# A bidirectional mixing layer with a mixture of experts: the first adaLN vectors summed in four parts with three projection units accumulating behind them, and gate units with the activations stationary

## The chip, the cores and the metric

One core of a Trainium2 chip runs the whole layer. The metric is the device time of one execution in microseconds (us), the median of several runs. TensorE (PE) multiplies matrices, VectorE (DVE) and ScalarE (ACT) do elementwise work, GpSimd (POOL) helps in two places, and SyncE (SP) issues nearly all loads from HBM, in program order. TensorE's clock is granted at one of two levels, 1.2 or 2.4 GHz; the profile shows it as 0.50 or 1.00.

## The reference, cut to what matters

256 tokens, D = 2048, one layer, everything in float32.

```python
mod = c @ ada_w + ada_b                      # (1, 6*2048)
sh1, sc1, gt1, sh2, sc2, gt2 = split(mod, 6)
h = rmsnorm(x, norm1_g) * (1 + sc1) + sh1
u = h @ w_in                                 # columns: A 512, B 1024, C 1536, D 512, gates 4*2048
y_a = pool_mixer(u_A) * pool_scale; y_b = conformer(u_B); y_c = short_conv(u_C); y_d = fourier(u_D)
merged = sum_k sigmoid(gate_k) * y_k         # each y_k is 512 channels times a 512 x 2048 matrix
x = x + gt1 * (merged @ w_o)
h2 = rmsnorm(x, norm2_g) * (1 + sc2) + sh2
x = x + gt2 * moe(h2)     # 32 experts, top 2 of 8 in the best group of 4; w1, w3: 2048x512, w2: 512x2048
return rmsnorm(x, final_g)
```

## The kernel before

The order of the work on each engine is written out by hand, with a semaphore for each dependence; an engine's instructions and a queue's loads run strictly in the order in which they are written. `ring` is seven SBUF slots of 2 MB; loads of `w_in` and `ada_w` go through it.

**Head.** ACT issues sixteen small loads (`keep`, rows of norm and bias vectors, `c`), PE turns them into columns (L480 to L484), and SP's first `ada_w` load waits for the last of them. The vectors sh1 and sc1 are then made one after the other: SP loads `ada_w` in 16 tiles of 2 MB (two rows k of 2048 columns for each partition, runs of 8 KB), DVE multiplies each row by its element of `c` and adds it to `acc` (L1117, L1119: 16 instructions of 128x2048 for a vector), and PE sums `acc` over the partitions with 16 matmuls against ones (`sum_ada`, L503). Only when both vectors are there does ACT scale and shift `hT` (L913), 16 instructions, one for each 128 rows of the contraction.

**Projection units.** Seven units of 512 columns follow: five as `unit_T` (L523: the weights stationary, 256 tokens moving, output transposed), two as `unit_N` (L536: `hT` stationary, 512 columns of weights moving). A unit needs two tiles of `w_in` of 2 MB (eight rows of 512 columns for each partition, runs of 2 KB). A float32 matmul is recorded as two. DVE works behind them: more `ada_w` rows for gt1 and sh2, the 31-tap convolution (L1171, 120 instructions), the short convolution and a layer norm. Then come the DFT and the pooling on PE (L570 to L594).

**Gate units.** For each of four branches g, four units j of 512 gate columns in three fp32r products (high times high, high times low, low times high). `gate_unit` holds the weights stationary, `g_hi` for two of the three and `g_lo` for the third, and moves 256 tokens of `h_hi` or `h_lo` (L611, L613, L615): 192 matmuls a unit, in 8 pieces. For each piece ACT makes the high part of the weights (L975) and DVE the low part (L1242), three pieces ahead (`AHEAD`) and with four buffers for the high part. After a unit `gate_y` multiplies the branch's 512 channels with its output matrix (L587), DVE multiplies by the sigmoid and adds into `mergedT`. Meanwhile DVE sums further `ada_w` rows in tiles of 1 MB with two buffers (`ada_one`, L1234): sc2 during branch 0 (16 tiles over three units), gt2 during branches 1 and 2 (two tiles a unit). Branches 1 and 2 are one hardware loop (`Fori`) on every engine. SP's order is: a weight tile, two `ada_w` tiles, a weight tile, and so on.

**Output projection, router and experts.** `wo_products` (L686 to L688) multiplies `mergedT` with `w_o`, in 32 pieces, again three products; here the activations are stationary and 512 columns of weights move. The residual, the second norm and a router of many small steps on DVE follow. For the experts, the tokens are split into three bf16 parts (`xparts`, ACT L1020 and L1032, POOL L470) and gathered by matmul with 0/1 selection matrices (`gather`, L758: `xparts_k` stationary, read with a step of 16 elements). 32 passes, one for each expert; a pass loads 12 tiles of 1 MB (`in_exp_w`).

## Time and profile before

| | |
|---|---|
| median of 3 runs | 1986.92 us (1986.51 to 1989.77) |
| profiled execution | 1989.88 us; its span from first to last instruction 1988.1 us |
| busy | PE 1815.1 us (91%), DVE 729.1 us, ACT 424.3 us, POOL 16.8 us |
| DMA | 641.11 MB, mean 322 GB/s |
| mean granted clock of PE | 0.951 |

Read it by stages, since these have different limits: the head ends at 115.2 us, the third projection unit at 200.2, the seventh at 319.2, the first gate unit starts at 336.25, branch 0 ends at 459.2, branch 1 at 581.2, branch 2 at 710.6, branch 3 at 836.4, the output projection at 929.6, and the first pass of the experts starts at 994.0.

### The profile page before, as it was taken

The page shows a single profiled execution, that of the slowest core. Times are in us where ns is not written, and L with a number is a line of the kernel's source. Part 1 is how long each engine was busy: PE and PEld are TensorE (multiplying, and loading weights), DVE is VectorE, ACT ScalarE, POOL GpSimd, SP SyncE. Part 2 cuts the span into 40 slices and gives each one's busy share as a digit, 9 for nine tenths or more (in the row PEclk, how much of TensorE's full clock was granted, in tenths as well). Part 3 has the DMA queues.
Part 4 walks back from the last instruction along what each step waited for, and adds up shares of the span by engine and source line. Part 5 has one row for each costly group of instructions (what it writes and reads, how often), then busy time and mean ns, then how long its engine had stood idle before and what let it go on. Part 6 is the DMA issues. An engine that isn't in the chain of part 4 may idle for free.

```text
span 1988.1 us, 28852 instructions
## 1 busy us (share of the span) xinstructions
PE 1815.1 (91%) x11742; PEld 1233.8 (62%) x11742; DVE 729.1 (37%) x824; ACT 424.3 (21%) x506; POOL 16.8 (1%) x7
## 2 busy tenths in 40 slices
PE   1189999999999999997399999999999999999987
PEld 1178855998999999886245454544545445445444
DVE  5848855585545634444611111111111111111113
ACT  3020003332323323334111111111111111111112
POOL 0000000000000000000300000000000000000000
PEclk8589999998999999998699999999999999999999
DMA  8998676497565644455099999999999999999971
GB/s 364 419 367 329 239 294 250 156 399 292 218 249 206 259 170 170 160 194 208 5 380 422 422 422 422 422 422 422 422 422 422 422 422 422 422 422 422 422 333 64
DMA packets 128765, 641.11 MB, mean 322 GB/s; under 512 B 12944, under 2 KB 13380, under 8 KB 64196
## 3 DMA queue, kind: packets, MB, share of 16 engines
q1 hardware_dynamic: 127568, 638.12, 79.4%
q0 software_dynamic: 144, 1.70, 0.2%
q8 instruction: 46, 0.75, 0.1%
q10 hardware_dynamic: 996, 0.44, 0.1%
q14 instruction: 11, 0.09, 0.0%
HBM read 638.14 MB, written 2.10 MB: 322 GB/s over the span
## 4 chain that ended last, share of the span: by engine, by line
PE 70%; DMA 21%; DVE 6%; issue 1%; ACT 1%; ACTq 0%; SPq 0%; DVEq 0%
DMA ring<-in_exp_w 17%; PE ps L802 16%; PE ps L523 7%; PE ps L780 7%; PE ps L758 6%; PE ps L611 5%; PE ps L613 5%; PE ps L615 5%; PE ps L587 4%; DMA ring<-in_ada_w 4%; PE ps L536 3%; DVE r_m L1119 2%; PE ps L868 1%; PE ps L686 1%; PE ps L687 1%; PE ps L688 1%
## 5 line engine op out<-in xcount | busy, mean ns | idle before, releaser
L802 PE MATMUL ps<-ring 128*64 128x512 f32 x2048 | 468.1, 599 | 8.4 <-DMA ring<-in_exp_w 5.0
L802 PEld LDWEIGHTS ps<-ring 128*64 128x64 f32 x2048 | 151.1, 137 | 270.9 <-issue 265.7
L615 PE MATMUL ps<-h_hi,g_lo 128*128 128x256 f32 x1024 | 293.6, 287 | 0.0
L1481 DVE TENSOR_TENSOR r_c<-ps,scale 128x512 f32<-128x512 f32 x65 | 44.9, 691 | 535.4 <-PE ps L758 535.2
L758 PEld LDWEIGHTS ps<-r_c,xparts 128*128 128x128 bf16 x3120 | 199.6, 168 | 58.6 <-issue 51.1
L611 PE MATMUL ps<-h_hi,mix_hi 128*128 128x256 f32 x768 | 224.5, 292 | 6.8 <-DVE g_lo L1242 3.7
L613 PE MATMUL ps<-h_lo,mix_hi 128*128 128x256 f32 x768 | 221.3, 288 | 0.0
L758 PE MATMUL ps<-r_c,xparts 128*128 128x64 bf16 x3120 | 206.6, 228 | 7.3 <-ACT r_c L1034 5.2
L615 PEld LDWEIGHTS ps<-h_hi,g_lo 128*128 128x128 f32 x1024 | 200.6, 196 | 0.0
L975 ACT ACTIVATE mix_hi<-ring 128x1024 fp32r<-128x1024 f32 x96 | 101.3, 1059 | 276.1 <-PE ps L615 263.4
L611 PEld LDWEIGHTS ps<-h_hi,mix_hi 128*128 128x128 f32 x768 | 151.8, 198 | 8.2 <-DVE g_lo L1242 4.3
L1119 DVE SCALAR_TENSOR_TENSOR r_m<-ring,ccol,r_m 128x2048 f32<-128x2048 f32 x60 | 141.1, 2352 | 39.5 <-DMA ring<-in_ada_w 37.9
L1242 DVE TENSOR_TENSOR g_lo<-ring,mix_hi 128x1024 fp32r<-128x1024 f32 x96 | 117.2, 1225 | 98.8 <-ACT mix_hi L975 96.3
L613 PEld LDWEIGHTS ps<-h_lo,mix_hi 128*128 128x128 f32 x768 | 151.7, 198 | 0.4
L523 PE MATMUL ps<-r_h,ring 128*128 128x256 f32 x640 | 140.4, 383 | 1.4 <-ACT r_h L913 1.4
L1059 ACT ACTIVATE ring<-ps 128x512 f32<-128x512 f32 x64 | 34.7, 595 | 471.5 <-PE ps L780 471.5
L523 PEld LDWEIGHTS ps<-r_h,ring 128*128 128x128 f32 x640 | 122.9, 192 | 18.4 <-issue 1.4
L780 PE MATMUL ps<-ring,r_c 128*64 128x512 f32 x512 | 119.2, 607 | 3.1 <-DVE r_c L1498 3.1
L780 PE MATMUL ps<-r_b,r_c 128*64 128x512 f32 x512 | 116.9, 598 | 0.0
L1490 DVE TENSOR_TENSOR r_m<-ps,mod 128x512 f32 x64 | 41.2, 687 | 203.0 <-PE ps L790 203.0
L587 PE MATMUL ps<-r_b,ring 128*128 (+1 forms) x416 | 94.3, 384 | 0.3 <-DVE mod L1156 0.3
L780 PEld LDWEIGHTS ps<-ring,r_c 128*64 128x64 f32 x512 | 40.8, 139 | 79.9 <-issue 79.9
(247 smaller groups left out, 1675.4 us busy)
## 6 DMA issues: line engine op xcount, KB each, us to landing
ring<-in_exp_w SPq DMA_DIRECT2D x320, 1024.0 KB, 21.1
ring<-in_w_in SPq DMA_DIRECT2D x46, 2048.0 KB, 8.9
ring<-in_ada_w SPq DMA_DIRECT2D x32, 2048.0 KB, 11.8
r_b<-in_exp_w SPq DMA_DIRECT2D x64, 1024.0 KB, 21.2
ring<-in_ada_w SPq DMA_DIRECT2D x32, 1024.0 KB, 9.0
ring<-in_w_o SPq DMA_DIRECT2D x8, 2048.0 KB, 7.6
ring<-in_branch_w SPq DMA_DIRECT2D x6, 2048.0 KB, 10.7
r_m<-in_x SPq DMA_DIRECT2D x1, 2048.0 KB, 12.9
```

The costliest lines, as they stand in the source:

```text
L523: last = mm(u[:, f, :], w[:, kk, f * P:(f + 1) * P], hT[:, k, :], start=(k == 0 and f % 2 == 0), stop=(k == KT - 1), skip_group_check=True)
L536: last = mm(ps[:, u_bank(n) + t, :], hT[:, k, t * P:(t + 1) * P], w[:, kk, :], start=(k == 0), stop=(k == KT - 1))
L587: last = mm(y[:, f, :], lhs(k, f), rhs(k), start=(k == 0), stop=(k == kts - 1))
L611: mm(u[:, f, :], hi[:, o:o + P], h_hi[:, k, :], start=(k == 0 and f % 2 == 0), stop=False, skip_group_check=True)
L613: mm(u[:, f, :], hi[:, o:o + P], h_lo[:, k, :], start=False, stop=False, skip_group_check=True)
L615: last = mm(u[:, f, :], lo[:, o:o + P], h_hi[:, k, :], start=False, stop=(k == KT - 1), skip_group_check=True)
L758: last = mm(gat[:, kk, :], xparts_k[:, i, t, k, :], sel_e[:, t, :], start=(t == 0 and i == 0), stop=(t == TT - 1 and i == 2))
L780: last = mm(ps[side * NWIN:(side + 1) * NWIN, 4 + b, :], hid[:, f, :], chunk(CHUNKS + f)[:, q * MIX:(q + 1) * MIX], start=(f == 0), stop=( ...
L802: last = mm(ps[m * NWIN:(m + 1) * NWIN, 2, :], xe[:, k, :], chunk(2 * c + m)[:, kk * F:(kk + 1) * F], start=(k == 0), stop=(k == KT - 1))
L975: A(g_hi[x % 4], slot(q % W_SLOTS)[:, (x % 4) * 1024:(x % 4 + 1) * 1024], ACT.Copy).then_inc(g_hi_done, 1)
L1119: ins = V.scalar_tensor_tensor(out=acc, in0=w[:, i, :], scalar=ccol[:, kk:kk + 1], in1=acc, op0=ALU.mult, op1=ALU.add)
L1242: V.tensor_tensor(g_lo[:, q, (x % 4) * 1024:(x % 4 + 1) * 1024], slot(q)[:, (x % 4) * 1024:(x % 4 + 1) * 1024], g_hi[x % 4].bitcast(F32), ...
```

## The change

1. **Small loads.** The host lays out all small vectors as columns; ACT issues three small loads and the load of x. SP's first instruction is an `ada_w` load, with no wait. The transposes of the small vectors go.
2. **The first shift and scale in four parts.** sh1 and sc1 are made for 512 columns at a time: for each part, SP loads four `ada_w` tiles of 2 MB (eight rows of 512 columns, runs of 2 KB) and then three `w_in` tiles of 1 MB (four rows of 512 columns). DVE runs 32 instructions of 128x512 for a part, PE sums, DVE adds the bias, ACT modulates four k, and PE adds these four k to three projection units, held in PSUM at once.
3. **What follows in the projection.** Four units are left. gt1 is made there (8 tiles of 2 MB), sh2, sc2 and gt2 are made one in each of branches 0, 1 and 2, 16 tiles of 1 MB each, four in a unit.
4. **Gate units.** `h_hi` and `h_lo` are stationary and 512 columns of weights move: 96 matmuls a unit. `gate_y` likewise moves 512 columns. The merged result therefore stands with the tokens on the partitions, and is turned on PE (`turn_merged`, 8 transposes for each j) before the output projection. `pool_scale` is multiplied into `pool_w` on DVE (128x2048), which the first `gate_y` waits for. The row of gt1 is made in two halves.
5. **Loops.** PE, DVE and SP write branches 1 and 2 out; ACT keeps its loop.
6. **Gather.** `xparts` is written with a step, so that `gather` reads 128 neighbouring elements.

```diff
-            sp.dma_start(x_in, x_v).then_inc(x_loaded, 16)
-            sp.wait_ge(const_in, 16 * 16)
-            for n in range(ADA0):
-                if n >= ADA_FIRST:
-                    sp.wait_ge(acc_step, 2 * (n - ADA_FIRST + 1))
-                load_ada(n // 8, n % 8, 3 + n % ADA_FIRST, ada_in[n % ADA_FIRST])
+            def load_head(part, v, half):
+                i = 4 * part + 2 * v + half
+                if i >= ADA_FIRST:
+                    sp.wait_ge(acc_step, 8 * (i - ADA_FIRST + 1))
+                sp.dma_start(slot(3 + i % ADA_FIRST).rearrange("p (k n) -> p k n", k=8),
+                             ada_v[:, 8 * half:8 * half + 8, v * D + part * PART:v * D + (part + 1) * PART]
+                             ).then_inc(ada_in[i % ADA_FIRST], 16)
+            for part in range(4):
+                for v in range(2):
+                    for half in range(2):
+                        load_head(part, v, half)
+                for n in range(HEAD):
+                    load_head_w(part, n)
+            load_unit(3, 0)
...
+            load_gt1(2)
+            load_gt1(3)
+            load_gt1(4)
             gate_w(0, 0)
...
+            for part in range(4):                       # PE
+                head_sums(part)
+                for n in range(HEAD):
+                    u = tiles((0, 4, 2)[n])
+                    for kk in range(4):
+                        k = 4 * part + kk
+                        if n == 0:
+                            pe.wait_ge(h_ready, k + 1)
+                        for f in range(4):
+                            last = mm(u[:, f, :], head_w(i)[:, kk, f * P:(f + 1) * P], hT[:, k, :], ...)
+                    last.then_inc(head_used, 1)
...
-                        for f in range(4):
-                            o = kk * MIX + f * P
-                            mm(u[:, f, :], hi[:, o:o + P], h_hi[:, k, :], ...)
-                            mm(u[:, f, :], hi[:, o:o + P], h_lo[:, k, :], ...)
-                            last = mm(u[:, f, :], lo[:, o:o + P], h_hi[:, k, :], ...)
+                        cols = slice(kk * MIX, (kk + 1) * MIX)
+                        for t in range(TT):
+                            h = h_hi[:, k, t * P:(t + 1) * P]
+                            mm(ps[:, b + t, :], h, hi[:, cols], start=(k == 0), stop=False)
+                            mm(ps[:, b + t, :], h, lo[:, cols], start=False, stop=False)
+                            last = mm(ps[:, b + t, :], h_lo[:, k, t * P:(t + 1) * P], hi[:, cols], ...)
...
-                            last = mm(gat[:, kk, :], xparts_k[:, i, t, k, :], sel_e[:, t, :],
+                            last = mm(gat[:, kk, :], xparts[:, i, t, k * P:(k + 1) * P], sel_e[:, t, :],
...
-            A(xparts[:, 0, :, :], xn2, ACT.Copy).then_inc(parts_act, 1)
+            A(xparts_q[:, 0, :, :, :], xn2_q, ACT.Copy).then_inc(parts_act, 1)
...
+                for vec in range(2):                    # DVE, for each part
+                    total = head_acc(part, vec)
+                    for k in range(KT):
...
+                            ins = V.scalar_tensor_tensor(out=total, in0=w, scalar=ccol[:, k:k + 1], in1=total, ...)
+                        ins.then_inc(acc_step, 1)
+                        v.wait_ge(acc_step, 32 * part + 16 * vec + k + 1)
...
-            ADA_AT = {8 + 3 * k // 2: (k,) for k in range(16)}
...
+                    if i % 2 == 1:
+                        ada_one(0, 4 * j + i // 2)
                 if j == 0:
-                    save_mod(SH2, y_bank(n))
+                    v.wait_ge(bw_in, 16)
+                    v.wait_ge(ps_in, 16)
+                    V.tensor_tensor(slot(BW)[:, 0:2048], slot(BW)[:, 0:2048], slot(BW)[:, 2048:4096], ALU.mult
+                                    ).then_inc(pw_ready, 1)
...
-            with v.Fori(1, N_BRANCH - 1) as g:
+            for g in range(1, N_BRANCH - 1):
                 branch_gate(g, False)
...
+                    if g == N_BRANCH - 1 and j > 0:     # PE
+                        turn_merged(j - 1)
+            pe.wait_ge(row_saved, 1)
+            gate_row(1)
+            pe.wait_ge(row_saved, 2)
```

## Rows read from the trace of the kernel before

**Rows 1.** Busy time by stage: length, PE, PEld, DVE, ACT, POOL, clock, DMA share, GB/s.
```profile
40.00:85.00 45.00, 6.96 (x32) 6.90 (x32) 36.47 (x18) 0.00 (x0) 0.00 (x0) 0.50 1.01 422
95.00:116.00 21.00, 7.74 (x34) 7.62 (x35) 13.21 (x8) 1.53 (x4) 0.00 (x0) 0.50 1.04 388
115.20:200.20 85.00, 84.98 (x385) 74.55 (x386) 55.92 (x81) 9.55 (x17) 0.00 (x0) 0.98 0.85 335
200.20:319.20 119.00, 119.00 (x434) 80.25 (x433) 80.54 (x98) 8.16 (x11) 0.00 (x0) 0.99 0.76 291
319.20:336.25 17.05, 13.73 (x48) 8.74 (x46) 5.91 (x6) 10.89 (x11) 0.00 (x0) 1.00 0.66 248
336.25:459.20 122.95, 117.33 (x865) 115.10 (x865) 82.89 (x67) 40.16 (x39) 0.00 (x0) 0.92 0.68 262
459.20:581.20 122.00, 121.97 (x897) 118.29 (x896) 66.33 (x48) 37.54 (x36) 0.00 (x0) 0.98 0.62 236
581.20:710.60 129.40, 126.60 (x928) 123.19 (x928) 69.20 (x50) 37.54 (x36) 0.00 (x0) 0.97 0.62 234
710.60:836.40 125.80, 125.55 (x905) 120.33 (x905) 49.71 (x41) 42.25 (x40) 0.00 (x0) 0.98 0.42 155
836.40:929.60 93.20, 89.60 (x386) 73.02 (x384) 50.53 (x49) 32.77 (x31) 0.00 (x0) 0.98 0.53 194
1520.00:1920.00 400.00, 393.76 (x2745) 195.22 (x2741) 59.62 (x93) 65.35 (x93) 0.00 (x0) 1.00 1.01 422
```

**Rows 2.** Timeline of the head: start, length, engine, line, operation [idle before it].
```profile
13.64 1.91 ACT L898 ACTIVATE r_b<-r_m 128x2048 f32<-128x2048 f32 x1 [2.35 <-DMA r_m<-in_x]
...
70.98 35.78 DVE L1119 SCALAR_TENSOR_TENSOR r_m<-ring,ccol,r_m 128x2048 f32<-128x2048 f32 x15
```

**Rows 3.** Groups of DVE and ACT by form: count, busy us, mean ns, idle before.
```profile
L1119 DVE SCALAR_TENSOR_TENSOR r_m<-ring,ccol,r_m 128x2048 f32<-128x2048 f32 x60 | 141.1, 2352 | 39.5 <-DMA ring<-in_ada_w 37.9 <-DVE r_b L1171 0.2
L1457 DVE SCALAR_TENSOR_TENSOR r_c<-r_m,rs,r_c 128x512 bf16<-128x512 f32 x2 | 1.5, 751 | 0.1
L1242 DVE TENSOR_TENSOR g_lo<-ring,mix_hi 128x1024 fp32r<-128x1024 f32 x96 | 117.2, 1225 | 98.8 <-ACT mix_hi L975 96.3
L975 ACT ACTIVATE mix_hi<-ring 128x1024 fp32r<-128x1024 f32 x96 | 101.3, 1059 | 276.1 <-PE ps L615 263.4
```

**Rows 4.** Timeline: neighbouring matmuls of a gate unit (256 columns), then of the output projection (512).
```profile
342.05 0.28 PE L615 MATMUL ps<-h_hi,g_lo 128*128 128x256 f32 x1
342.17 0.28 PE L611 MATMUL ps<-h_hi,mix_hi 128*128 128x256 f32 x1
...
884.33 0.39 PE L686 MATMUL ps<-mix_hi,m_hi 128*128 128x512 f32 x1
884.56 0.39 PE L687 MATMUL ps<-g_lo,m_hi 128*128 128x512 f32 x1
```

**Rows 5.** Chain of waits within branch 0: start, length, what.
```profile
404.06 2.36 DVE r_m L1234
406.44 7.94 DMA ring<-in_ada_w
```

**Rows 6.** Chain of waits where the loop goes from branch 1 to branch 2.
```profile
574.26 6.91 PE ps L587 x32
581.17 2.82 issue
...
585.00 0.21 PE ps L611
```

**Rows 7.** Timeline from the second norm to the first gather.
```profile
938.83 3.62 ACT L1020 ACTIVATE xparts<-r_b 128x4096 bf16<-128x4096 f32 x1
...
938.94 5.10 PE L715 MATMUL ps<-keep,r_b 128*128 128x128 f32 x32 [9.31 <-ACT r_b L1016]
...
960.63 7.93 POOL L470 TENSOR_TENSOR xparts<-r_b,xparts 128x4096 bf16<-128x4096 f32 x1 [8.49 <-ACT xparts L1032]
...
981.65 3.23 PE L758 MATMUL ps<-r_c,xparts 128*128 128x64 bf16 x48 [5.25 <-ACT r_c L1034]
```

More of the change, by code:

```diff
@@ L65, with build @@
 N_MIXC = 1024 * 3 + 256
-def build(nc, x, c, ada_w, ada_b, norm1_g, w_in, pool_w, pool_scale, conf_dw_w, conf_dw_b, conf_ln_g,
-          conf_ln_b, branch_w, sc_conv_w, w_o, norm2_g, rg_w, rg_b, re_w, re_b, exp_w1, exp_w3,
-          exp_w2, final_g, keep_consts, mix_consts, iota_const, out):
+def build(nc, x, ada_w, w_in, pool_w, pool_scale, branch_w, w_o, rg_w, re_w, exp_w1, exp_w3, exp_w2, final_g,
+          columns, router_b, keep_consts, mix_consts, iota_const, out):
     with ExitStack() as ctx:
@@ L342, in gate_w @@
+            load_unit(3, 0)
+            load_unit(3, 1)
+            load_unit(4, 0)
+            load_gt1(0)
+            load_unit(4, 1)
+            load_gt1(1)
+            for n in (5, 6):
+                for half in range(2):
+                    load_unit(n, half)
             def gate_w(g, x):
                 q = G0 + x
-                if isinstance(g, int) and x < W_SLOTS and g == 0:
-                    sp.wait_ge(w_used, q - W_SLOTS + 1)
+                if x < W_SLOTS and g == 0:
+                    sp.wait_ge(w_used, q - 6)
@@ L496, in _ @@
             acc_k = acc.rearrange("p (q k) -> p k q", k=KT)
-            def sum_ada(n, bank):
-                pe.wait_ge(acc_step, 16 * (n + 1))
-                for k in range(KT):
-                    part = acc_k[:, k, :] if n == SH2 else acc[:, k * P:(k + 1) * P]
-                    last = mm(ps[:, bank, k:k + 1], part, ones[:, 0:1], start=True, stop=True)
-                last.then_inc(summed, 1)
-            pe.wait_ge(xT_saved, 8)
-            sum_ada(SH1, 2)
-            pe.wait_ge(mod_ready, 1)
@@ L509, in _, with head_sums @@
-            sum_ada(SC1, 2)
-            def unit_T(n, loaded):
+            def head_sums(part):
+                for v in range(2):
+                    pe.wait_ge(acc_step, 16 * (2 * part + v + 1))
+                    for kk in range(4):
+                        o = 16 * v + 4 * part + kk
+                        last = mm(ps[:, 6 + v, o:o + 1], head_acc(part, v)[:, kk * P:(kk + 1) * P], ones[:, 0:1],
+                                  start=True, stop=True)
+                    last.then_inc(summed, 1)
@@ L595, in _ @@
             last.then_inc(dft_done, 1)
+            pe.wait_ge(acc_step, ADA1)
+            for k in range(KT):
+                last = mm(ps[:, 6, k:k + 1], acc[:, k * P:(k + 1) * P], ones[:, 0:1], start=True, stop=True)
+            last.then_inc(summed, 1)
             def gate_unit(g, j):
-                u = tiles(u_bank(N_UNIT + j))
+                b = u_bank(N_UNIT + j)
                 for i in range(GATE_PIECES):
@@ L1601 @@
         a = _np.asarray(given[name])
-        if name not in ("final_g", "branch_w"):
+        if name not in ("final_g", "branch_w", "columns", "router_b"):
             a = a[0]
```

524 lines of the change are left out of this document (261 added, 263 removed).

## The prediction

> **What bounds the kernel now.** I read the stages first, then the timeline of the head, then the chain of waits inside the gate units, and last the experts.
>
> The stages [rows 1] show four different limits. In the head the core loads at full rate (DMA share 1.01) while PE has 6.96 us of work in 45: nothing multiplies until both vectors exist. From 115.2 to 319.2 us PE is busy without a gap, so there the number and length of its matmuls is the limit, and DVE and DMA have room. In branch 0 the DMA share and DVE's load are high and the clock is 0.92; the chain alternates between an `ada_w` tile that takes 7.94 us to land and the 2.36 us that DVE spends on it, 10.3 us for two tiles [rows 5]. In branches 1 to 3 PE is busy all the time again, except where the loop turns: 2.82 us of issue, and then matmuls of 0.21 us where a full clock gives 0.12 [rows 6, 4]. In the experts DMA stands at share 1.01 and 422 GB/s with PE at 393.76 of 400 us [rows 1]: a pass loads 12 tiles of 1 MB, 12.58 MB, and at 422 GB/s that is 29.8 us. So the expert stage ends a fixed time after its first loads can start; a faster PE there gives nothing, and whatever is won must be won before it.
>
> **Head and projection: 46 us.** *Loads.* Up to the last `ada_w` tile of part four there are 16 tiles of 2.097 MB and nine `w_in` tiles of 1.049 MB, 43.0 MB, all in runs of 2 KB. Runs of 2 KB went at 388 GB/s where they were alone at a full queue (95 to 116 us), runs of 8 KB at 422 [rows 1]. I take 388: 110.8 us. Ahead of or between them come x and the constants, 4.2 MB, 10 us, and a start at 1 us: the last tile lands at 122, the first of part four at 106. *DVE.* An instruction of 128x2048 takes 2.352 us, 15 of them 35.78, a gap of 0.03 [rows 2, 3]; one of 128x512 took 0.751 [rows 3]. 32 a part at 0.78 are 25.1 us, 100 in all, against 74 before: more DVE work, because each instruction is a quarter as long but carries the same fixed part. x landed at 13.6 us beside one other load [rows 2]; now three queues share, so I put it at 15.5 and the first sum at 20, after ACT's two squares (1.91 each) and two small steps. Parts one to three then wait for tiles (a part's 11.5 MB take 29.7 us, DVE 25 and 2 for the exchange with PE), so part four starts when its tile lands, 106, and ends at 131. *Hand-over.* Four sums at half clock 1.7 (6.96 for 32 records [rows 1]), three small DVE steps 0.7, one ACT instruction 0.6: PE starts at 134. *PE.* 48 matmuls, 96 records, at 85.0/385 = 0.221 us [rows 1]: 21.2 us. After the idle time some of it will run at half clock; the loop's turn cost 5.8 us of which 2.8 were idle, so about 3 [rows 6]; I take 2.5. Three units are done at 157.5. Before it was 200.2, so 42.7 us. Parts one to three are hidden: PE's 24 us fit into 29.7. The `w_in` tiles of a part reuse slots that PE freed two parts, some 50 us, earlier (`head_used`), so SP is not held up there, and the tiles of the fourth unit land by 150.
>
> By the Trainium skill ("DMA: Bandwidth & Descriptors", Specifications) transfers of 512 B and more run at line rate, so runs of 2 KB should cost nothing. The rows at 388 and 422 speak against it, and I keep the measured rate; what the rule would make of the time stands among the rivals.
>
> *Rest of the projection.* 119.0 us before, of which 3.5 (half of 6.96, at the full clock) were the sum for gt1, which moves behind the DFT: 115.5. Then 17 us of DFT and pooling as before, in whose last 3.3 us PE waited for the first pieces, and the moved sum fits there. The first gate unit starts at 157.5 + 115.5 + 17 = 290 instead of 336.25: 46 us. DVE's work here: convolution from 6 us before the third unit's end, 49 us, done before PE asks at 55; then five and three gt1 tiles of 4.8 us with two buffers, each refilled in about 7.6 us, done 111 us after the third unit, 5 before PE's last unit ends. Those 5 us are the cover; SP's `gate_w(0, 0)` and `gate_w(0, 1)` stand behind `load_gt1(4)` and `load_gt1(6)` and come with 15 us to spare. If the chain is late, the split of h waits (`acc_step`, ADA1) and the first gate unit with it, one for one.
>
> **Gate units.** The spacing of matmuls is 0.12 us for 256 columns and 0.23 (0.227 over longer stretches, 87 us for the 384 of the output projection) for 512 [rows 4]. A unit goes from 192 x 0.12 = 23.0 to 96 x 0.227 = 21.8. The form with 512 columns and stationary activations is the one that the output projection already runs, so both prices are of the same products. `gate_y` stays at 6.9 us [rows 6] (16 matmuls of 256 or 8 of 512), 1.7 in branch 0.
> *Branch 0:* 4 x (21.8 + 1.7) = 94. The scaling of `pool_w` is new: DVE comes to it after piece 7 of the first unit, ACT's 1.06 and DVE's 1.23 for one piece more [rows 3], an `ada_w` row 2.35 and the scaling itself, twice 1.225: 7.2 us, of which PE's last piece covers 2.7. PE waits 4.5, and after it and at the start about 2.3 each at half clock; behind it stand `gate_y` and the next unit. The final sum 3.5: 107 in all. Could the tiles hold it up as before? Two tiles now fall on four pieces and half a `gate_y`, 11.7 us, where the chain needs 10.3 [rows 5]; before they fell on three pieces. So PE sets the pace by 1.4 us per pair. 123.0 to 107: 16 us.
> *Branches 1 and 2:* 4 x (21.8 + 6.9) + 3.5 = 118.3 each, against 122.0 and 129.4 [rows 1]: the second loses the loop's turn as well (5.8). 14.8 us. DVE has eight pieces, four rows and 2.4 of merging, 21.8 us, in 28.7; the loads 9.4 MB, 24 us at 388.
> *Branch 3:* 114.8, three times eight transposes at 5.10/32 [rows 7], 1.3 each, half the row of gt1 1.7: 120.4 against 125.8, 5.4 us.
> *Output projection:* 93.2, less 1.2 of waiting for the merged result, plus the second half of the row 1.7, its copy 1.3 before PE may go on, a turn 1.3: 96.3, a loss of 3. SP's loads of router weights now wait for this row, and the fourth `w_o` tile stands behind them; it comes some 8 us later and was some 16 early, so nothing.
>
> **Gather, router, experts: nothing.** The two gathers ahead of the first pass take about 3.2 us each [rows 7], where 48 x 64 columns at the lower clock of 1.2 GHz alone are 2.6: at most 1.2 us to win. The copies into `xparts` now write with a step: ACT's 3.62 us, POOL's 7.93 twice [rows 7]. POOL's second subtraction ends at 968.6 and the first gather starts at 981.65, since it also waits for the selection: 13 us of cover. Below: minus 1.2. Above: ACT twice as long, 3.6 on the path to the router, and POOL half as long again, 4 us twice, which its cover holds. I take nothing. In the Trainium skill the page "SBUF — State Buffer" (Door 1: The DMA port swizzle, the note on 16-byte lines) says that an access which goes to a new line each time pays. That speaks for the gather and against the copies, and no row here shows an ACT or POOL write with a step; by it the sum would be 4 us worse.
>
> **Sum.** 46 + 16 + 14.8 + 5.4 - 3 = 79.2. The profiled execution, 1989.9 (span 1988.1), would be 1910.7; it lay 3 us above the median of the runs, so the median goes from 1986.9 to **1908**.
>
> **The rivals.**
> 1. *The loads of the head run at 422* (the rule above, as a mechanism of this kernel: 43.0 MB in 102 us). Then DVE binds: 20 + 4 x 25.1 + 3 x 2 = 126 instead of 131, and the result is 1903. For it: other stretches reach 422; against it: the 21 us at 388. 12%.
> 2. *Branch 0 keeps the pace of its loads.* The 1.4 us of room per pair go when the `w_in` tile ahead of each pair is slower or DVE comes late; PE then waits and falls to half clock, as in [rows 1], 0.92. Its 16 us are not won: 1924. For it: the chain before is just this, and 16 rows must now be done in a branch that has 17 us less. 14%.
> 3. *The copies with a step cost.* 4 to 8 us, 1914. 10%.
> 4. *gt1 comes late* at the end of the projection, by 5 to 10 us beyond its cover: 1915. 6%.
> 5. *PE stays at half clock in the head*, because it works in bursts: 96 x 0.427 = 41 us a part and 3 of exchange, more than the loads' 29.7, so the three units end at 47 + 4 x 44 = 223 instead of 157.5, and the result is 1974. Against it: the units began at full clock at once after 7 us of small sums, and the bursts are 70% of the time. 3%.
> 6. *Slower than before: the gather's new weight reads cost more, not less.* It is in every pass, 96 matmuls of 0.067 us at the first one [rows 7]. The loads cover up to 0.5 us a pass [rows 1]; to lose 79 us over 31 passes takes 2.5 more, so the point is 0.10 us a matmul. At 0.13 a pass is 35.5 us, 5.7 over the loads, and the result 2085. No row speaks for it but that the form is not in the trace. 3%.
> That the change does not do what it says would be head matmuls waiting for all four parts; the waits on `h_ready` and `mod_ready` go part by part, so I give it nothing of its own.
>
> **How the numbers follow.** Forecast 50%, by itself 1898 to 1920 (head 4 us better to 8 worse, waits of the gate units 6 either way). With the rivals above, 2% for the rest. Below 1894 only rate and waits together could lead; above 1934 lie rivals 5 and 6 and two of the others at once. A change under 0.2%, 4 us, cannot be told from none here. Faster 96%, same 1%, slower 3%.
>
> **What the profile after will show.** Step by step: DVE's group of 128x512 at 0.75 us in the head and 388 GB/s there; ACT's first scaled rows of part four at 134 us; the third unit's end at 157; the first gate matmul at 290; 0.227 us between gate matmuls; a wait of 4.5 us of PE on the scaled `pool_w`; no 2.8 us of issue between branches; the first expert pass at about 915; 422 GB/s from there to the end. It is wrong if the clock in the head is 0.5 while matmuls run, if the chain in branch 0 still names `in_ada_w`, or if PE waits for nothing in a pass of the experts.

## The result, and the profile after

The changed kernel takes 1952.92 us (median of 4 runs, 1952.59 to 1953.35), where the kernel before takes 1988.30 on the same chip (4 runs, 1986.51 to 1989.77): a ratio of 0.9821, with an interval of 0.9807 to 0.9834. It is faster by 35.4 us. The forecast was 1908, a gain of 79; its own range ended at 1920, and that with most of the rivals at 1934. The sign was right and less than half of the gain came.

The profiled run took 1952.59 us, its span is 1950.8. These are its stages, in the columns of [rows 1], cut where the same piece of work ends:

```profile
20.00:106.00 86.00, 58.75 (x272) 52.22 (x272) 71.87 (x106) 16.26 (x24) 0.00 (x0) 0.85 1.05 387
134.90:160.10 25.20, 23.96 (x97) 20.62 (x98) 7.03 (x18) 4.38 (x6) 0.00 (x0) 0.86 0.76 287
160.10:273.70 113.60, 113.60 (x402) 75.96 (x401) 90.02 (x145) 8.16 (x10) 0.00 (x0) 1.00 0.73 276
290.90:400.00 109.10, 104.50 (x434) 83.47 (x434) 83.38 (x56) 40.40 (x39) 0.00 (x0) 0.95 0.81 300
400.00:528.20 128.20, 124.45 (x482) 92.84 (x482) 83.93 (x57) 37.62 (x36) 0.00 (x0) 0.97 0.81 302
528.20:651.00 122.80, 120.23 (x481) 88.80 (x481) 83.93 (x57) 37.63 (x36) 0.00 (x0) 0.99 0.80 296
651.00:771.70 120.70, 120.70 (x478) 88.82 (x478) 52.33 (x43) 40.40 (x39) 0.00 (x0) 0.99 0.44 161
771.70:867.70 96.00, 90.53 (x396) 73.07 (x395) 48.35 (x47) 34.70 (x33) 0.00 (x0) 1.00 0.53 191
867.70:959.30 91.60, 26.55 (x194) 19.78 (x195) 28.91 (x105) 51.00 (x23) 29.27 (x2) 0.62 0.13 49
959.30:1950.80 991.50, 893.25 (x6608) 387.83 (x6608) 157.77 (x242) 168.01 (x246) 0.00 (x0) 0.98 0.96 399
```

Read it against the forecast from the top. The loads of the head ran at 387 GB/s, the third unit ended at 160.1, and the first gate unit began at 290.9 instead of 336.25 [rows 1]: 45.4 us won where 46 were forecast. Branch 0 takes 109.1 us, branch 3 120.7, the output projection 96.0, each within 2 us of its forecast. Two stretches are off. Branches 1 and 2 take 128.2 and 122.8 us instead of 118.3 each. And the stretch from the end of the output projection to the first expert matmul takes 91.6 us, which I had left as it was; before it lasted 64.4, from the end of the last stage but one in [rows 1], 929.6, to an expert matmul that starts at 993.99. Against the forecast for the profiled run, 1910.7, the 41.9 us are made up like this:

| stretch | forecast | measured | off by |
|---|---|---|---|
| start to first gate matmul | 290.0 | 290.9 | +0.9 |
| branch 0 | 107 | 109.1 | +2.1 |
| branches 1 and 2 | 236.6 | 251.0 | +14.4 |
| branch 3, output projection | 216.7 | 216.7 | 0 |
| second norm to first expert matmul | 64.4 | 91.6 | +27.2 |
| first expert matmul to the end | 994.1 | 991.5 | -2.6 |

The timeline of ScalarE and GpSimd shows where the largest term is; the rows that answer to them are in [rows 7]:

```profile
876.89 18.65 ACT L1068 ACTIVATE xparts<-r_b 128x4096 bf16<-128x4096 f32 x1
895.03 3.88 ACT L1072 ACTIVATE r_m<-ps,mod,scale 128x256 f32<-128x256 f32 x8
...
911.10 18.39 ACT L1080 ACTIVATE xparts<-r_b 128x4096 bf16<-128x4096 f32 x1
...
895.62 10.85 POOL L501 TENSOR_TENSOR r_b<-r_b,xparts 128x4096 f32<-128x4096 f32 x1 [893.71 <-ACT xparts L1068]
929.57 18.42 POOL L503 TENSOR_TENSOR xparts<-r_b,xparts 128x4096 bf16<-128x4096 f32 x1 [23.10 <-ACT xparts L1080]
```

ScalarE's copy of 128x4096 takes 18.65 us where it took 3.62, five times as long for the same elements and types: only the step of the write is new. GpSimd's second subtraction takes 18.42 instead of 7.93. The first copy also stands ahead of ScalarE's eight instructions that prepare the router's input (L1072), so the router starts later. The chain of waits names the same instructions, one behind the other:

```profile
876.89 18.66 ACT xparts L1068
895.54 0.07 issue
895.62 10.85 POOL r_b L501
906.47 23.07 issue
929.53 18.47 POOLq L73
...
959.31 5.95 PE ps L866 x13
```

The 23.07 us of "issue" are GpSimd waiting for ScalarE's second copy. That copy starts at 911.10, 4.6 us after the first subtraction has ended at 906.47: it stands on ScalarE behind a small instruction (L1078) that waits for VectorE's router.

For branches 1 and 2 the chain of waits at the start of branch 1 is the row to read:

```profile
392.94 7.07 PE ps L679 x32
...
413.10 2.27 DVE r_m L1281
415.39 0.33 SPq L397
415.76 11.09 DMA ring<-in_branch_w
426.90 7.13 PE ps L617 x16
```

The half of `branch_w` that the branch's first product needs is issued at 415.76 and lands at 426.85. Its slot was free since PE's last product of branch 0 ended, at 392.6. But SP is an engine with one queue, and ahead of this load stand rows of `ada_w` that wait for VectorE (`DVE r_m L1281`). The same happens for each half of `branch_w` in branches 1 and 2, four times, the load going out 13 to 23 us after its slot was free: 6.3 us of PE's idle time, and after each wait a product of 7.13 us where 6.87 is usual. The granted clock stays at 1.00 there. The first row is another surprise, the closing sum of a branch: 32 records in 7.07 us, where the forecast had 3.5.

The experts are as before: in them PE waits for `in_exp_w` 63 times, 80.6 us, so a faster gather there can't show.

### The profile page after: what moved, and what is told of

Read it like the earlier page. It is cut to its first block, busy times and chain, and to the rows that moved or that the text cites. A ratio compares the mean times of both kernels' runs of the same rounds, so it can differ in the third digit from the quotient of the medians.

```text
span 1950.8 us, 25208 instructions
## 1 busy us (share of the span) xinstructions
PE 1718.7 (88%) x10026; PEld 1017.7 (52%) x10026; DVE 741.0 (38%) x915; ACT 454.7 (23%) x507; POOL 30.2 (2%) x7
## 4 chain that ended last, share of the span: by engine, by line
PE 48%; DMA 39%; DVE 6%; ACT 2%; issue 2%; POOLq 1%; SPq 1%; POOL 1%; ACTq 0%; DVEq 0%
DMA ring<-in_exp_w 34%; PE ps L866 10%; PE ps L647 5%; PE ps L648 5%; PE ps L649 5%; PE ps L617 5%; DVE r_m L1183 4%; PE ps L560 3%; PE ps L573 3%; DMA ring<-in_branch_w 2%; PE ps L844 2%; DMA ring<-in_ada_w 2%; PE ps L932 1%; PE ps L742 1%; PE ps L744 1%
## 5 line engine op out<-in xcount | busy, mean ns | idle before, releaser
L866 PE MATMUL ps<-ring 128*64 128x512 f32 x2048 | 486.2, 618 | 82.9 <-DMA ring<-in_exp_w 80.6
L648 PE MATMUL ps<-g_lo,h_hi 128*128 128x512 f32 x512 | 201.9, 394 | 0.0
L647 PE MATMUL ps<-mix_hi,h_hi 128*128 128x512 f32 x384 | 158.2, 412 | 0.0
L649 PE MATMUL ps<-mix_hi,h_lo 128*128 128x512 f32 x384 | 151.8, 395 | 0.0
L822 PEld LDWEIGHTS ps<-r_c,xparts 128*128 128x128 bf16 x3120 | 96.0, 99 | 78.6 <-issue 75.7
L822 PE MATMUL ps<-r_c,xparts 128*128 128x64 bf16 x3120 | 103.8, 194 | 26.9 <-POOL xparts L503 24.2
L648 PEld LDWEIGHTS ps<-g_lo,h_hi 128*128 128x128 f32 x512 | 97.9, 191 | 23.1 <-issue 3.2
L1281 DVE SCALAR_TENSOR_TENSOR r_m<-ring,col,r_m 128x2048 f32<-128x2048 f32 x45 | 105.5, 2344 | 0.0
L617 PE MATMUL ps<-ring,r_b 128*128 128x512 f32 x208 | 94.2, 604 | 10.6 <-DMA ring<-in_branch_w 6.3
L1183 DVE SCALAR_TENSOR_TENSOR r_m<-ring,col,r_m 128x512 f32<-128x512 f32 x120 | 90.2, 752 | 4.3
L647 PEld LDWEIGHTS ps<-mix_hi,h_hi 128*128 128x128 f32 x384 | 74.0, 193 | 18.2 <-issue 2.7
## 6 DMA issues: line engine op xcount, KB each, us to landing
ring<-in_exp_w SPq DMA_DIRECT2D x320, 1024.0 KB, 23.6
```

Of the source, the lines that this page charges most:

```text
L617: last = mm(ps[:, y_bank(n) + t, :], lhs(k, t), rhs(k), start=(k == 0), stop=(k == kts - 1))
L647: mm(ps[:, b + t, :], h, hi[:, cols], start=(k == 0), stop=False)
L648: mm(ps[:, b + t, :], h, lo[:, cols], start=False, stop=False)
L649: last = mm(ps[:, b + t, :], h_lo[:, k, t * P:(t + 1) * P], hi[:, cols], start=False, stop=(k == KT - 1))
L822: last = mm(gat[:, kk, :], xparts[:, i, t, k * P:(k + 1) * P], sel_e[:, t, :], start=(t == 0 and i == 0), stop=(t == TT - 1 and i == 2))
L866: last = mm(ps[m * NWIN:(m + 1) * NWIN, 2, :], xe[:, k, :], chunk(2 * c + m)[:, kk * F:(kk + 1) * F], start=(k == 0), stop=(k == KT - 1))
```

## The experiments

Every kernel was compared with the kernel before on the same chip; its medians there were 1988.5, 1989.0 and 1988.0 for the three groups of four. "Gap" is the time from the start of ScalarE's first copy into `xparts` to the first expert matmul, read from each trace.

| kernel | time, us | copies of ScalarE | subtractions of GpSimd | gap |
|---|---|---|---|---|
| before | 1988.3 | 3.62, 3.60 | 7.94, 7.93 | 55.2 |
| after | 1952.9 | 18.65, 18.39 | 10.85, 18.42 | 82.4 |
| e4, before with the copies with a step and the gather contiguous | 2015.0 | 18.63, 18.39 | 10.86, 18.42 | 82.5 |
| e1, after with the old copies and gather | 1928.6 | 3.62, 3.60 | 7.94, 7.93 | 55.9 |
| e2, after, all four walk by the output | 1928.6 | 7.16, 7.07 | 10.24, 9.89 | 59.9 |
| e7, ScalarE's two walk by the output | 1940.5 | 7.16, 7.05 | 10.86, 18.43 | 68.8 |
| e11, GpSimd's two walk by the output | 1945.2 | 18.66, 18.40 | 10.18, 9.90 | 73.9 |
| e5, e1 with the earlier load of e3 | 1921.0 | 3.62, 3.60 | 7.94, 7.93 | 56.2 |
| e6, e5 with GpSimd in eight pieces | 1916.7 | 3.62, 3.60 | 7.94, 9.04 | 52.2 |
| e12, before with the eight pieces | 1984.2 | 3.62, 3.60 | 7.94, 9.04 | 53.0 |

**The copies undone (e1).** Theory A was that the writes with a step are the 27 us; its rival that the stretch is longer for other reasons and the copies cost the 4 to 8 us of the forecast's rival 3.

```diff
-            A(xparts_q[:, 0, :, :, :], xn2_q, ACT.Copy).then_inc(parts_act, 1)
+            A(xparts[:, 0, :, :], xn2, ACT.Copy).then_inc(parts_act, 1)
```

and likewise the second copy, both subtractions and the gather, which reads with a step again.

> The changed kernel with one part of the change undone: the parts of xn2 for the gather are written and read in the old order (contiguous copies, gather weights with a step). Theory A, the writes with a step hold up the first expert pass: ScalarE's two copies fall from 18.6 and 18.4 to 3.6 us each, GpSimd's two subtractions from 10.9 and 18.5 to about 8 each, the first expert pass starts about 27 us sooner (932 instead of 959) and the time is 1926 (1922 to 1930). Rival, the 27 us come from elsewhere (router weights that land later behind the second half of the gt1 row, or a half clock) and the copies cost only the 4 to 8 us of the forecast: 1945 to 1949. Second rival, the gather's strided weight reads matter in the passes now that PE is closer to the loads: 1930 or more although the first pass starts at 932.

1928.59 us, ratio 0.9693 (0.9677 to 0.971). The gap is 55.9 us again, 26.5 less, and the first expert matmul starts at 935.9. 24.3 us came back: theory A holds, and the first rival falls. The second is nearly nothing: from the first expert matmul to the end the kernels whose gather reads with a step took 990.5 to 994.1 us, those with contiguous weights 989.8 to 991.7, on average 2 us less over 32 passes.

**The same part of the change alone, on the kernel before (e4).**

```diff
-            A(xparts[:, 0, :, :], xn2, ACT.Copy).then_inc(parts_act, 1)
+            A(xparts_q[:, 0, :, :, :], xn2_q, ACT.Copy).then_inc(parts_act, 1)
```

> The kernel before with one part of the change alone: copies into the gather parts with a step, gather weights contiguous. Theory A: the first pass starts at 1021 instead of 994 and the time is 2015 (2010 to 2020), while the gathers themselves get no faster in the end because the loads bind. Rival (forecast): 4 to 8 us, 1992 to 1996. Second rival: the contiguous gather weights win time in each of 32 passes, so that less than 20 us are lost.

2014.96 us, ratio 1.0136 (1.0117 to 1.0156): 26.5 us slower than before. The gap grew by 27.3 us. So the cost doesn't depend on the rest of the change, and the gather with contiguous weights gives back little in all its passes.

**The step moved from the write to the read (e2).** The layout of `xparts` stays as in the change, and the instructions walk through it in its own order:

```diff
-        xparts_q = xparts[:, :, :, :].rearrange("p i t (k q) -> p i t q k", k=KT)
+        xparts_q = xparts[:, :, :, :].rearrange("p i t (k q) -> p i t k q", k=KT)
-        xn2_q = r_b[:, :].rearrange("p (t q k) -> p t q k", t=TT, k=KT)
+        xn2_q = r_b[:, :].rearrange("p (t q k) -> p t k q", t=TT, k=KT)
```

> The changed kernel with the same contraction-major parts, but the copies and subtractions walk them in the order of the output: the bf16 side is contiguous and the float32 side has a step of 64 bytes. Theory A1, the write step of 256 bytes alone is dear: ScalarE 4 to 6 us a copy, 1926 to 1932. Theory A2, any step of 64 bytes or more costs the same on either side: ScalarE 18 us a copy, GpSimd slower still since its first subtraction now has a step on two operands of float32, 1950 to 1960.

1928.62 us, ratio 0.9695 (0.9679 to 0.9711):

```profile
876.75 7.16 ACT L1068 ACTIVATE xparts<-r_b 128x4096 bf16<-128x4096 f32 x1
...
883.99 10.24 POOL L501 TENSOR_TENSOR r_b<-r_b,xparts 128x4096 f32<-128x4096 f32 x1 [882.08 <-ACT xparts L1068]
905.25 9.89 POOL L503 TENSOR_TENSOR xparts<-r_b,xparts 128x4096 bf16<-128x4096 f32 x1 [11.02 <-ACT xparts L1080]
```

The same elements in the same places, and ScalarE needs 7.16 us instead of 18.65. Reading float32 with a step of 64 bytes costs it a factor of 2, writing bf16 with a step of 256 bytes a factor of 5. That is theory A1, though 7.2 us lies above the 4 to 6 expected of it.

**Which engine carries it (e7, e11).** Two kernels, each with the walk of only one engine turned round.

```diff
-            A(xparts_q[:, 0, :, :, :], xn2_q, ACT.Copy).then_inc(parts_act, 1)
+            A(xparts_r[:, 0, :, :, :], xn2_r, ACT.Copy).then_inc(parts_act, 1)
```

> The changed kernel with ScalarE's two copies walking in the order of the output (7.2 and 7.1 us) and GpSimd's two subtractions as in the change (10.9 and 18.5 us), which tells ScalarE's share of the 27 us. Theory A: the four instructions are a chain with some 13 us of cover at its end; it gets 22.7 us shorter, and then the router's own path (copies to first pass) is about level with it, 1928 to 1932. Rival A3, GpSimd's 18.5 us on the last link is what costs most: 1940 to 1945.

1940.46 us, ratio 0.976 (0.9744 to 0.9777). Theory A was wrong here, and so was its picture of 13 us of cover at the end of the chain; the time lies in the range of rival A3. The timeline tells why. First GpSimd's second subtraction, then VectorE:

```profile
905.32 18.43 POOL L505 TENSOR_TENSOR xparts<-r_b,xparts 128x4096 bf16<-128x4096 f32 x1 [11.01 <-ACT xparts L1082]
...
905.68 0.14 DVE L1470 TENSOR_SCALAR ec<-ec 32x1 f32<-32x1 f32 x1
905.86 17.93 DVE L1472 TENSOR_SCALAR eh<-keep,ec 32x39 f32<-32x39 f32 x1
923.82 0.23 DVE L1474 TENSOR_SCALAR eh<-eh,ec 32x39 f32<-32x39 f32 x1
...
924.61 0.29 DVE L1472 TENSOR_SCALAR eh<-keep,ec 32x39 f32<-32x39 f32 x1
```

A VectorE instruction that takes 0.29 us a moment later takes 17.93, and it ends at 923.79, just after GpSimd's ends at 923.75. The trace shows no semaphore that it waited for. VectorE was held as long as GpSimd's instruction ran, and VectorE was computing the router's table, which is the path. So what I had called cover for GpSimd's second subtraction is work that stops if the subtraction runs beside it. The Trainium skill says so ("SBUF — State Buffer", Who interferes with whom): the two engines share a port pair as an exclusive lock for a whole instruction, when VectorE's has two inputs in SBUF or runs in one of the modes that use both ports. The trace agrees; the prediction should have used it. In the changed kernel itself VectorE is not held, since ScalarE's second copy ends at 929.5, after VectorE has finished the table at 928.8. The trace of before has the hold, 6.80 us on the instruction of line 1412. In e1, whose GpSimd instructions are those of before, it stands at line 1451:

```profile
902.97 7.93 POOL L503 TENSOR_TENSOR xparts<-r_b,xparts 128x4096 bf16<-128x4096 f32 x1 [8.49 <-ACT xparts L1080]
...
904.17 6.80 DVE L1451 TENSOR_SCALAR ct<-ct 32x128 f32<-32x128 f32 x1
911.01 0.59 DVE L1453 SCALAR_TENSOR_TENSOR ct<-ct 32x128 f32<-32x128 f32 x2
```

The counterpart changed GpSimd's walk alone:

```diff
-            nc.gpsimd.tensor_tensor(xn2_q, xn2_q, xparts_q[:, 0, :, :, :], ALU.subtract).then_inc(parts_sub, 1)
+            nc.gpsimd.tensor_tensor(xn2_r, xn2_r, xparts_r[:, 0, :, :, :], ALU.subtract).then_inc(parts_sub, 1)
```

> The changed kernel with GpSimd's two subtractions walking in the order of the output (10.2 and 9.9 us) and ScalarE's two copies as in the change (18.6 and 18.4 us): the counterpart of the run with ScalarE's copies alone changed. The four instructions are a chain again (57 us) and it gets 9.3 us shorter; the first pass starts at 950 and the time is 1944 (1941 to 1947). Rival: ScalarE's first copy holds up the router itself by 12 us and nothing changes while it does, 1950 or more.

1945.16 us, ratio 0.9777 (0.9759 to 0.9796), as theory A said. Here ScalarE's second copy ends so late that VectorE has finished its table and waits for GpSimd's result:

```profile
940.77 0.55 DVE L1507 TENSOR_SCALAR r_b<-r_m,rs 128x512 f32<-128x512 f32 x1 [10.83 <-POOL xparts L505]
```

The gap is 8.5 us shorter, the 8.5 of the second subtraction (18.42 to 9.90). The first, 0.7 shorter, counts for nothing: as in the changed kernel it ends some 5 us before the second copy can start. So the path of the changed kernel is the first copy, the router's first half behind it on ScalarE, the second copy and the second subtraction; theory A's chain had one link too many. ScalarE's walk alone gives 12.5 us, GpSimd's 7.8, both 24.3: more than the sum of 20.3, since each, made short alone, still leaves VectorE waiting or held.

**GpSimd's subtraction in pieces (e6, e12).** If VectorE is held for the length of one GpSimd instruction, short instructions let it through.

```diff
-            nc.gpsimd.tensor_tensor(xparts[:, 2, :, :].rearrange(flat), r_b[:, :], xparts[:, 1, :, :].rearrange(flat), ALU.subtract
-                                    ).then_inc(parts_sub, 1)
+            for s in range(8):
+                cs = slice(512 * s, 512 * (s + 1))
+                nc.gpsimd.tensor_tensor(xparts[:, 2, :, :].rearrange(flat)[:, cs], r_b[:, cs],
+                                        xparts[:, 1, :, :].rearrange(flat)[:, cs], ALU.subtract).then_inc(parts_sub, 1)
```

> The kernel with both causes removed, and GpSimd's second subtraction cut into eight pieces of 128x512 instead of one of 128x4096. Theory C: while GpSimd runs the one long instruction a VectorE instruction on float32 in SBUF (0.21 us alone) can't end before it, 6.80 us in the trace of before; with pieces it gets through after one piece, about 1 us, 5 to 6 us go from the router's path and the time is 1915 (1913 to 1917). Rival: each later piece stops VectorE again, or the pieces cost GpSimd as much more as is won: 1919 to 1922.

1916.67 us (1914.82 to 1918.77), ratio 0.964 (0.9624 to 0.9656), 4.4 us less than the kernel with one long subtraction:

```profile
893.31 9.04 POOL L505 TENSOR_TENSOR xparts<-r_b,xparts 128x512 bf16<-128x512 f32 x8 [8.49 <-ACT xparts L1082]
...
894.51 1.13 DVE L1453 TENSOR_SCALAR ct<-ct 32x128 f32<-32x128 f32 x1
895.68 2.30 DVE L1455 SCALAR_TENSOR_TENSOR ct<-ct 32x128 f32<-32x128 f32 x2
```

GpSimd needs 1.1 us more, and VectorE is held five times for up to 1 us, 3.7 in all, instead of once for 6.6. Both theory C and its rival had a part of the truth: 5 to 6 us were expected. In the traces the stretch from the second copy to the first expert matmul went from 36.7 to 34.1 us, 2.6 less; what the medians show beyond it is within the spread of the runs.

The same edit on the kernel before:

> The kernel before, with GpSimd's second subtraction in eight pieces of 128x512. Theory C (VectorE held until a GpSimd instruction ends) says that the loss was there before the change: 4.4 us as measured on the changed kernel, 1984.5 (1983 to 1986). Rival, the 4.4 us came from something in the changed kernel: 1988.

1984.23 us (10 runs), ratio 0.998 (0.9968 to 0.9992): 3.8 us, as theory C said, and 3.5 in the stretch from the second copy to the first expert matmul. The loss was there before the change, and no line of [rows 7] shows it; only VectorE's rows do.

**The load of `branch_w` earlier (e3).** Theory B was that SP's order makes it late, the rival that VectorE or the loads set the pace of branches 1 and 2.

```diff
+                        if i == 1 and g > 0 and j % 2 == 0:
+                            sp.wait_ge(y_done, 4 * g + j)
+                            sp.dma_start(slot(BW).rearrange("p (k n) -> p k n", k=4),
+                                         br_v[g - 1, :, :, j * MIX:(j + 2) * MIX]).then_inc(bw_in, 16)
                         if g < N_BRANCH - 1:
                             ada_tiles(g, 4 * j + 2 * i, 2)
...
-                    if g > 0 and j % 2 == 0:
-                        sp.wait_ge(y_done, 4 * g + j)
-                        sp.dma_start(slot(BW).rearrange("p (k n) -> p k n", k=4),
-                                     br_v[g - 1, :, :, j * MIX:(j + 2) * MIX]).then_inc(bw_in, 16)
```

> The changed kernel with the load of branch_w issued ahead of the second pair of ada_w rows instead of behind it; nothing else moves. Theory B, in branches 1 and 2 PE waits because this load stands in SP's queue behind waits for DVE's rows: the four waits of PE on branch_w (6.3 us in all) and the half clock behind them go, branches 1 and 2 take 118 to 120 us each instead of 128.2 and 122.8, and the time is 1940 (1937 to 1944). Rival, DVE's pace or the loads' rate sets the length of these branches: the waits move to g_lo or ada_w, the branches stay within 2 us of 128 and 123, and the time is 1950 to 1954.

1944.76 us (1941.79 to 1946.29), ratio 0.9777 (0.9758 to 0.9796): 8.2 us won, where 9 to 16 were expected. PE has no wait on `branch_w` left, and the four products behind the waits take 6.87 us again, which makes 7.3 us; the half clock that was to come on top had never been behind these waits. The chain of waits now holds PE alone:

```profile
399.93 0.64 PE ps L647
...
423.50 6.87 PE ps L617 x16
...
452.14 6.87 PE ps L617 x16
...
516.29 6.72 PE ps L679 x32
...
546.48 6.87 PE ps L617 x16
...
639.26 3.76 PE ps L679 x32
```

From the end of one gate product (423.50 + 6.87) to the start of the next are 452.14 - 430.37 = 21.8 us, to the tenth what the forecast had for a unit. The first unit of a branch takes 23.6 (399.93 to 423.50), and the sum before it 6.72 us instead of 3.5 in one branch, 3.76 in the other. Branch 1 now takes 123.1 us and branch 2 120.0; what is left over 118.3 is the sum, which the next run looks into, and what follows it at the lower clock.

**The closing sum twice (e9).**

```diff
-                for k in range(KT):
+                for k in list(range(KT)) * 2:
```

> The changed kernel with the closing sum of branches 0 to 2 done twice (32 matmuls of one column instead of 16, three times; the result is the same). Theory E: during this sum of one-column matmuls the granted clock falls, so it costs 7 us (records of 0.355 us, half the speed of the 0.167 us seen elsewhere) and not the 3.5 of the forecast: three more sums cost some 21 us less what the waits behind them take back, 1971 (1967 to 1976). Rival, the clock falls at this point because of what came before, the wait on branch_w, and the second sum would run at full clock: 3 times 3.5, 1963 or less.

1977.59 us, ratio 0.9939 (0.9919 to 0.9959): 24.7 us slower than the changed kernel, where 1976 was the most expected. The chain of waits shows the three sums, of branches 0, 1 and 2:

```profile
392.86 14.00 PE ps L679 x64
...
529.37 13.65 PE ps L679 x64
...
665.86 9.78 PE ps L679 x64
```

The extra halves cost 6.9, 6.9 and 6.3 us, but not for one reason. Theory E took records of 0.355 us for a sign of the lower clock. In the changed kernel, one microsecond out of branch 0's sum and one out of branch 2's, in the columns of [rows 1], say otherwise:

```profile
393.00:394.00 1.00, 1.00 (x5) 1.00 (x6) 1.00 (x1) 0.00 (x0) 0.00 (x0) 1.00 1.22 401
648.00:649.00 1.00, 1.00 (x11) 1.00 (x11) 0.96 (x2) 0.00 (x0) 0.00 (x0) 1.00 0.42 41
```

Both are at full clock, and the first has half as many matmuls. For them the code differs in one thing: the sums of branches 0 and 1 read their stationary operand with a step of 16 floats, 64 bytes (`acc_k`), the sum of branch 2 reads it contiguous. With the step they run at about six records a microsecond whether the clock stands at 1.00 or, from 395 on, at 0.50. The kernel before had both forms too, the sum for gt1 contiguous and the sum for sh2 with the step, both begun at full clock:

```profile
258.80 3.63 PE L503 MATMUL ps<-keep,r_m 128*128 128x1 f32 x32
...
360.89 6.98 PE L503 MATMUL ps<-keep,r_m 128*128 128x1 f32 x32
```

So the 7 us of branches 0 and 1 are the price of the step. No run changed that layout alone; these rows are what the reading rests on.

The clock is in the third sum. In the changed kernel its 32 records took 3.48 us. Doubled, the further 32 take 6.3, and the granted clock, 1.00 up to 669, is 0.50 from 670. So the matmuls of one column do bring the clock down, and the next unit's first matmuls pay for it (0.43 us instead of 0.23 each, for 4 us), with or without the doubling. Another 4.9 us of the profiled run, which is 25.6 us longer than that of the changed kernel, were lost at `branch_w`: PE's waits grew from 6.3 to 7.8 us, and two of the products behind them took 8.83 us instead of 7.13. The rival falls with the third sum: there was no wait before it. For the first two neither theory had the cause.

**The gate products in the old form (e10).**

```diff
-                            mm(ps[:, b + t, :], h, hi[:, cols], start=(k == 0), stop=False)
+                            mm(u[:, f, :], hi[:, o:o + P], h_hi[:, k, :], start=(k == 0 and f % 2 == 0), stop=False,
+                               skip_group_check=True)
```

and the other two products likewise. The gates come out in the wrong order, so only the times up to the end of the output projection count.

> The changed kernel with the gate products in the form of before (weights stationary, 192 matmuls of 256 columns a unit instead of 96 of 512). The sums then lie transposed in PSUM and the gates come out wrong, and the routing with them, so only the time up to the end of the output projection is compared. Theory F: a unit takes 23.0 instead of 21.8 us; 16 units are 19 us, less what the waits in branches 1 and 2 (branch_w) take back, 14 to 19 us later at the end of the output projection (882 to 887 instead of 867.6). Rival, the pace of VectorE and the loads hides the difference: less than 8 us.

```profile
429.83 7.13 PE ps L617 x16
...
459.99 6.87 PE ps L617 x16
...
894.11 18.78 ACT xparts L1069
```

A unit takes 459.99 - 436.96 = 23.0 us, and the first copy after the output projection starts at 894.1 instead of 876.9: 17.2 us for 16 units, of the 19 by the length of a unit; PE's waits on `branch_w` fell from 6.3 to 2.7 us, as expected. The gates with h stationary are worth what the forecast gave them.

**The head's loads in long runs (e8).**

```diff
-                sp.dma_start(slot(3 + i % ADA_FIRST).rearrange("p (k n) -> p k n", k=8),
-                             ada_v[:, 8 * half:8 * half + 8, v * D + part * PART:v * D + (part + 1) * PART]
+                sp.dma_start(slot(3 + i % ADA_FIRST).rearrange("p (k n) -> p k n", k=2),
+                             ada_v[:, 4 * part + 2 * half:4 * part + 2 * half + 2, v * D:(v + 1) * D]
```

and the head's `w_in` tiles likewise.

> The changed kernel with the head's ada_w and w_in tiles taken from other rows of the same arrays, the same 2.1 and 1.05 MB each, but in runs of 8 KB instead of 2 KB. The first shift and scale and the first three units are thus computed from the wrong weights, and what follows (the routing too) with them, so only the head's own times are compared. Theory D, the run length sets the rate: up to 422 GB/s instead of 387 in the stretches 20 to 106 us; VectorE binds then, and the third unit ends at 153 to 156 instead of 160.1. Rival, the rate of 387 comes from the number or mixture of transfers in the queue: no change, 160.

```profile
20.00:47.00 27.00, 7.14 (x40) 6.87 (x40) 18.45 (x27) 13.73 (x16) 0.00 (x0) 0.89 1.01 422
47.00:76.00 29.00, 22.07 (x89) 19.06 (x90) 25.89 (x39) 2.08 (x4) 0.00 (x0) 0.75 1.01 421
```

422 GB/s instead of 387, with tiles of the same size in the same order; the third unit ends at 155.7 instead of 160.1, although VectorE's first sum starts 5 us later here (x lands later behind the faster tiles). From then on VectorE is busy without a wait for a load. Run length sets the rate, as theory D has it, and VectorE would bind next. The tiles also lie at other places in HBM, which this run does not separate from the length of the runs, though the kernel before has the same two rates with the same two lengths [rows 1]. Contrary to the rule of the Trainium skill ("DMA: Bandwidth & Descriptors", Specifications) that was rival 1, runs of 2 KB don't reach the line rate here.

**Both causes removed (e5).** The edits of e1 and e3 together.

> The changed kernel with the copies and gather of before and with branch_w ahead of the second pair of ada_w rows. If the two causes are independent their gains add: 1928.6 less 8.2, 1920.4 (1918 to 1923). Rival, the experts' loads or the router absorb the time won in the branches: 1925 or more.

1921.02 us (1919.84 to 1922.15), ratio 0.9662 (0.9646 to 0.9678). The gains of 24.3 and 8.2 add to 32.5, and 31.9 were measured. With the pieces of the other run, 1916.7, this is the fastest version found, 72 us under the kernel before on its chip (1989.0).

## Why the prediction was wrong

1. *Loads and VectorE in the head: right.* 387 GB/s for 388; the instruction of 128x512 took 0.752 us for 0.751. x landed at 18.2 instead of 15.5, and VectorE's first sum began at 22.6 instead of 20. The chain of waits runs from there through VectorE's sums and the slots that they free: the tile that part four waited for was issued at 92.06, when VectorE had freed its slot. That fits the 2.6 us by which the third unit came later than 157.5; no run tests it. Rival 1 fell with the 387. Rival 5 fell too, with a clock of 0.85 from 20 to 106 us, but an argument against it was misread: the units of the kernel before did not begin at full clock, it stood at 0.50 until 118 us.
2. *Rest of the projection: right.* The first gate unit at 290.9 for 290; gt1 was in time, rival 4 fell.
3. *Gate units, branch 0: right, 2 us off.* PE waited 4.3 us for the scaled `pool_w`, 4.5 were forecast, and the loads didn't hold it up: rival 2 fell. The 2 us are the closing sum, 7.07 for 3.5 (item 4), less what the rest did better.
4. *Branches 1 and 2: the step that failed is "4 x (21.8 + 6.9) + 3.5 = 118.3 each".* The two products were sized right, as e3 and e10 show. Two things were missing. I named SP's queue for `gate_w` and the router's weights, but for these branches I only added up bytes ("9.4 MB, 24 us at 388") and never asked when SP gets to the `branch_w` load: 8.2 us. And I took every closing sum at 3.5 us, half of the head's 6.96, as if the clock of 0.50 [rows 1] were all that made a sum long. That holds for a contiguous operand only; the sums of branches 0 and 1 read theirs with a step and take 7 us at full clock too, and the trace of the kernel before had such a sum at 360.89. In e3 the two branches are 6.5 us over the forecast, of which 3.2 is the sum of branch 1, and the rest about the two first units behind the sums, 23.6 us instead of 21.8, which begin at the lower clock.
5. *Branch 3 and output projection: right,* 120.7 and 96.0 for 120.4 and 96.3.
6. *Gather, router, experts: the step that failed, and most of the miss.* "Above: ACT twice as long ... and POOL half as long again, 4 us twice, which its cover holds. I take nothing." The bound was no bound. No row had a ScalarE or GpSimd write with a step, and ends of twice and one and a half were guesses. It is 5.2 times for ScalarE and 2.3 for GpSimd's second subtraction. The places of the instructions I had right: the first copy stands before the router, and the second half has cover. What failed is the size. The traces of before and after add up so: the first copy +15.0, all on the path; from its end to the second copy 15.6 for 14.5, +1.1; the first subtraction +2.9, of which nothing counts; the second copy and the second subtraction together 25.3 longer, against a cover of 13, so that the stretch from the second copy to the gather takes 37.0 for 24.7, +12.3; from there to the first expert matmul 11.2 for 12.3, -1.2. That is the 27.2. The cover itself was less than it looked: in the kernel before, VectorE is held for 6.6 us of it, and in e7, where VectorE still had work to do, for 17.6. Rival 3 had the right mechanism with 4 to 8 us, a quarter of its price, and 10%.
7. *The experts: right.* 991.5 us for 994.1, bound by the loads; rival 6 fell, and what the gather won (in e2 a gather behind the first expert matmuls takes 1.51 us, in e1 3.11) is nearly all hidden.

## What to carry to other kernels

Before a copy is given a step so that a later read may be contiguous, price both sides: here four instructions that run once became 43 us longer, 27 of them on the path, to shorten matmuls that a load covers anyway. If the layout must change, let the instruction walk in the order of its output and read with the step. A matmul's stationary operand has its price too: two sums that read it with a step took twice as long. Follow the loading queue as an engine of its own, instruction by instruction: a load's bytes may fit while its place behind someone else's wait doesn't. And an operation that no row shows has no upper bound at "twice"; leave the range open towards it or keep it out of the sum's certain terms.

## What the runs showed of the hardware

- A ScalarE copy of 128x4096 from float32 to bf16: 3.62 us contiguous, 7.16 with a read step of 64 bytes, 18.65 with a write step of 256 bytes.
- A GpSimd subtraction of 128x4096: 7.93 us contiguous, 9.89 with a float32 read step of 64 bytes, 18.42 with a step of 256 bytes on its bf16 input and output.
- A VectorE instruction of 0.29 us took 17.93 while one GpSimd instruction ran. Instructions of one element per partition passed during the same time (0.14 us).
- 16 float32 matmuls of one column (32 records) took 3.48 and 3.63 us at full clock with a contiguous stationary operand of 128x128, and 6.98 and 7.07, begun at full clock, with one read with a step of 64 bytes.
- In e9 the first 32 records of the last sum ran in 3.48 us after a gate product and the next 32 in 6.3: such matmuls bring the granted clock to its lower level, 1.2 GHz, without any idle time.
- Loads from HBM in runs of 2 KB: 387 GB/s; the same tiles in runs of 8 KB: 422.
